# Streaming encoder step on one core: dense turns of one column group, additions to x and sums of squares on GpSimd, norms worked by group

## The reference

```python
def rmsnorm(x, gain):
    x32 = x.astype(F32)
    y = x32 * lax.rsqrt(jnp.mean(x32 * x32, axis=-1, keepdims=True) + EPS)
    return (y * gain.astype(F32)).astype(x.dtype)
...
    for l in range(DEPTH):
        ... mixer_inputs(rmsnorm(xp, norm1[l]), w_in[l], pos_p, lower[l])
        oa = diff_attn_prompt(aq, ak, av, lam)
        ob = dsa_prompt(bq, iq, iw, bk, bv, ik)          # top-256 keys of each query
        sc, oc = hgrn2_prompt(cq, ck, cg, cv)
        xp = xp + merge_heads(oa, ob, oc, cgate, lam_init, a_norm[l], c_norm[l], w_out[l])
        h, fc = conv_ffn(rmsnorm(xp, norm2[l]), hist0, ffn_up[l], ffn_conv_w[l], ffn_conv_b[l], ffn_down[l])
        xp = xp + h
    y_prompt = rmsnorm(xp, final_norm)
```

## Time and profile before

| | us |
|---|---|
| median of 3 runs | 4510.31 (4510.25 to 4512.2) |
| the profiled execution's own time | 4511.78 |
| its span | 4510.0 |
| PE busy / DVE busy / ACT busy / POOL busy | 4080.2 / 2281.9 / 996.6 / 224.3 |
| mean granted clock of TensorE | 0.919 |

### The profile page before, as it was taken

One profiled execution on the slowest core, in us unless ns is written; L12 is line 12 of the kernel. 1 busy time (PEld: TensorE's weight loads), 2 busy tenths in 40 slices (PEclk: granted clock), 3 DMA queues, 4 the chain that ended last, 5 costly groups with the idle time before them and its releaser, 6 DMA issues.

```text
span 4510.0 us, 47853 instructions
## 1 busy us (share of the span) xinstructions
PE 4080.2 (90%) x19244; PEld 2705.0 (60%) x19244; DVE 2281.9 (51%) x4647; ACT 996.6 (22%) x2287; POOL 224.3 (5%) x172
## 2 busy tenths in 40 slices
PE   7888788998889999998999998997899998899998
PEld 6665446776767767773444444486767776644443
DVE  1833454597942454439635555298924555522222
ACT  1113222110113333221223222011123332210001
POOL 2200220000000003100000000400000000000000
PEclk9995788999999999899998989998999998899999
DMA  3321122211120212221221211331121111122222
GB/s 127 109 91 31 53 64 90 77 66 47 52 84 18 69 61 73 87 84 70 70 74 49 73 56 55 108 110 56 45 79 54 47 55 56 37 85 65 77 75 73
DMA packets 142165, 310.33 MB, mean 69 GB/s; under 512 B 29160, under 2 KB 69608, under 8 KB 130680
## 3 DMA queue, kind: packets, MB, share of 16 engines
q1 hardware_dynamic: 81432, 262.25, 17.7%
q10 hardware_dynamic: 60512, 45.02, 3.5%
HBM read 271.08 MB, written 36.14 MB: 68 GB/s over the span
## 4 chain that ended last, share of the span: by engine, by line
PE 73%; DVE 19%; ACT 3%; issue 2%; DMA 1%; ACTq 1%; SPq 0%; DVEq 0%
PE PS L600 49%; PE PS L607 6%; DVE scr L1227 5%; DVE top L1226 5%; PE PS L698 4%; PE PS L687 3%; PE PS L671 3%; PE PS L657 2%; PE PS L576 2%; PE PS L794 1%; PE PS L725 1%; PE PS L793 1%; DVE inv L1164 1%; ACT scr L989 1%; DVE xn L1167 1%
## 5 line engine op out<-in xcount | busy, mean ns | idle before, releaser
L600 PE MATMUL PS<-xn,wring 128*128 128x272 f32 (+1 forms) x6048 | 1906.8, 477 | 74.1 <-DVE xn L1167 48.6
L600 PEld LDWEIGHTS PS<-xn,wring 128*128 128x128 f32 x6048 | 1188.2, 198 | 748.1 <-issue 552.6
L600 PE MATMUL PS<-dense,wring 128*128 128x272 f32 (+1 forms) x2112 | 681.3, 482 | 55.3 <-DVE xT L1173 45.9
L600 PEld LDWEIGHTS PS<-dense,wring 128*128 128x128 f32 x2112 | 417.2, 201 | 288.2 <-issue 217.2
L1173 DVE TENSOR_TENSOR xT<-PS,xT 128x272 f32<-128x272 f32 (+1 forms) x240 | 123.4, 523 | 499.0 <-PE PS L600 497.9
L1226 DVE MAX8 top<-scr 128x8 f32<-128x384 f32 (+6 forms) x418 | 367.5, 879 | 12.7
L1227 DVE MATCH_REPLACE8 scr<-top,scr 128x384 f32<-128x384 f32 (+6 forms) x418 | 359.9, 861 | 0.0
L607 PE MATMUL PS<-wring,xn 128*128 128x224 f32 (+1 forms) x1728 | 350.1, 364 | 10.5 <-ACT dense L865 10.5
L607 PEld LDWEIGHTS PS<-wring,xn 128*128 128x128 f32 (+1 forms) x1728 | 318.0, 187 | 35.5 <-ACT dense L865 11.2
L698 PE MATMUL PS<-kv,scr 128*128 128x64 f32 (+2 forms) x1804 | 249.5, 289 | 14.9 <-ACT scr L989 14.9
L698 PEld LDWEIGHTS PS<-kv,scr 128*128 128x128 f32 (+2 forms) x1804 | 237.6, 202 | 33.8 <-ACT scr L989 21.3
(11 more groups left out here) (160 smaller groups left out, 3090.8 us busy)
## 6 DMA issues: line engine op xcount, KB each, us to landing
wring<-in_wu SPq DMA_DIRECT2D x88, 1024.0 KB, 4.8
wring<-in_wf SPq DMA_DIRECT2D x76, 512.0 KB, 3.3
wring<-in_wd SPq DMA_DIRECT2D x64, 384.0 KB, 3.1
wring<-in_wn SPq DMA_DIRECT2D x24, 896.0 KB, 4.9
wring<-in_wd SPq DMA_DIRECT2D x64, 320.0 KB, 2.9
wring<-in_wo SPq DMA_DIRECT2D x32, 512.0 KB, 3.3
kv<-out_projT ACTq DMA_DIRECT2D x48, 256.0 KB, 4.3
out_projN<-dense SPq DMA_DIRECT2D x96, 112.0 KB, 1.7
```

The source lines that it names most:

```text
L600: mm = nc.tensor.matmul(PS[:, dbank(t.g0 + j), 0:cw], wtile(t.q, i), rhs, start=(kk == a), stop=(kk == b - 1))
```

## The change

- A turn works one column group (`j`), in both halves, and h = 1 is cut in two groups of 256.
- `f` begins with tiles 0, 1, 2 for group 0, then for group 1; later tiles take both groups in a row. `wo` and `dn` of pass 3 take all eight tiles for group 0 and then again for group 1, so that their weight tiles are loaded twice.
- ACT empties the banks of `wo` and `dn` as well, into two slots `res`; GpSimd adds them to x. In `wo` and in pass 3 of `dn`, GpSimd also squares the new x and adds the squares up over the eight tiles (in two tiles of `xn` that are free then). PE multiplies that one tile with a matrix of 1/1024. The norms at the start of P00 and P01 still square all eight tiles on ACT, now into `catT` (`direct`).
- The norm of group 0 stands before turn 3 of group 1 of the turns that add to x, and that of group 1 behind the first turn of the next stage that reads group 0.
- SP loads the 1/1024 matrix and the first half of x first, then three weight tiles, and then the constants and the other half.
- `LEAD` (dense turns ahead of the first mixer step) goes from 12 to 22, and a lag of 3 or 4 turns to 6, in a list of 974 turns where there were 542. `tout` has two slots where it had three.

```diff
-GRP = (((0, 272), (272, 272)), ((0, 512),))
+GRP = (((0, 272), (272, 272)), ((0, 256), (256, 256)))
+GMAX = 272
...
-NW, WSLOT = 3, 2048
+NW, WSLOT, NRES, NTO = 3, 2048, 2, 2
...
+def _norm(l, h, which, j, direct=0):
+    _turn("nsq", l, h, which, direct, j)
+    _turn("nsc", l, h, which, direct, j, ng=0)
...
 def _project(l, h):
-    _norm(l, h, 0)
-    for n in range(NPT):
-        _turn("f", l, h, n, load=("f", l, h, n, 0))
+
+    if l == 0:
+        _norm(l, h, 0, 0, 1)
+    for n, j in ((0, 0), (1, 0), (2, 0), (0, 1), (1, 1), (2, 1)) + tuple((n, j) for n in range(3, NPT) for j in range(2)):
+        _turn("f", l, h, n, 0, j, load=("f", l, h, n, 0))
+        if (n, j) == (0, 0):
+            _norm(l, h, 0, 1, 1 - l)
...
+def _added(kind, l, h, p, norm):
+
+    for j in range(2):
+        for n in range(KD):
+            _turn(kind, l, h, n, p, j, load=(kind, l, h, n, p))
+            if (n, j) == (2, 1):
+                _norm(*norm, 0)
 
 
 def _ffn(l, h):
-    for n in range(KD):
-        _turn("wo", l, h, n, load=("wo", l, h, n, 0))
-    _norm(l, h, 1)
-    ups = iter(range(NF))
+    _added("wo", l, h, 0, (l, h, 1))
     for p, upto in enumerate((8, 14, 19, 22)):
         for n in range(upto):
             if n >= (0, 8, 14, 19)[p]:
-                _turn("a", l, h, n, load=("u", l, h, n, 0))
-                _turn("g", l, h, n, load=("u", l, h, n, 0))
-        for n in range(KD):
-            _turn("dn", l, h, n, p, load=("dn", l, h, n, p))
+                order = ("a", 0), ("a", 1), ("g", 0), ("g", 1)
+                for kind, j in (("a", 0), ("g", 0), ("a", 1), ("g", 1)) if n == 0 else order:
+                    _turn(kind, l, h, n, 0, j, load=("u", l, h, n, 0))
+                    if (kind, n, j) == ("a", 0, 0):
+                        _norm(l, h, 1, 1)
+        if p < 3:
+            for n in range(KD):
+                for j in range(2):
+                    _turn("dn", l, h, n, p, j, load=("dn", l, h, n, p))
+    _added("dn", l, h, 3, (1, h, 0) if l == 0 else (L, h, 2))
...
 def _finish(h):
-    _norm(L, h, 2)
+    _norm(L, h, 2, 1)
     _turn("y", L, h, ng=0)
...
         def bank_free(pe, g):
-            if g >= 2:
-                by, n = EMPTIED[g - 2]
-                pe.wait_ge(s_ea if by == "act" else s_ed, n)
+            pe.wait_ge(s_ea, max(0, g - 1))
...
-            for t, name in ((ident, "ident"), (ones, "ones"), (lmask, "lmask"), (bmask, "bmask"), (fgain, "fgain"), (clow, "clow"),
-                            (par, "params")):
-                sp.eng.dma_start(t[:], io[name]).then_inc(s_const, 16)
-            sp.eng.dma_start(scr[:, 0:256].rearrange("p (l c) -> p l c", l=L), io["lam"]).then_inc(s_const, 16)
+            sp.eng.dma_start(mean[:], io["mean"]).then_inc(s_mean, 16)
             for k in range(KD):
-                sp.eng.dma_start(xT[:, k, :], io["xT"][k * P:(k + 1) * P, :]).then_inc(s_x, 16)
+                sp.eng.dma_start(xT[:, k, 0:W[0]], io["xT"][k * P:(k + 1) * P, 0:W[0]]).then_inc(s_x[0][k], 16)
+
+            def load_rest():
+                for t, name in ((par, "params"), (fgain, "fgain"), (clow, "clow"), (ident, "ident"), (lmask, "lmask"), (bmask, "bmask")):
+                    sp.eng.dma_start(t[:], io[name]).then_inc(s_const, 16)
+                sp.eng.dma_start(scr[:, 0:256].rearrange("p (l c) -> p l c", l=L), io["lam"]).then_inc(s_const, 16)
+                for k in range(KD):
+                    sp.eng.dma_start(xT[:, k, C0[1]:T], io["xT"][k * P:(k + 1) * P, C0[1]:T]).then_inc(s_x[1][k], 16)
...
-                    N = norm_index(k)
-                    for kk in range(KD):
-                        pe.wait_ge(s_sq, KD * N + kk + 1)
-                        for j, (c, cw) in enumerate(GRP[t.h]):
-                            if kk == 0:
-                                bank_free(pe, t.g0 + j)
-                            mm = nc.tensor.matmul(PS[:, dbank(t.g0 + j), 0:cw], ones[:], sq[:, kk % 2, c:c + cw],
-                                                  start=(kk == 0), stop=(kk == KD - 1))
-                            if kk == KD - 1:
-                                mm.then_inc(s_mm, 1)
-                        if kk < KD - 1:
-                            mm.then_inc(s_sqf, 1)
+                    c, cw = GRP[t.h][t.j]
+                    out = PS[:, dbank(t.g0), 0:cw]
+                    bank_free(pe, t.g0)
+                    if t.p:
+                        for kk in range(KD):
+                            pe.wait_ge(s_sq, KD * norms_before(k) + kk + 1)
+                            mm = nc.tensor.matmul(out, mean[:], catT[:, kk, c:c + cw], start=(kk == 0), stop=(kk == KD - 1))
+                    else:
+                        pe.wait_ge(s_acc, norms_before(k) - 4 + 1)
+                        mm = nc.tensor.matmul(out, mean[:], xn[:, SUM, c:c + cw], start=True, stop=True)
+                    mm.then_inc(s_mm, 1)
...
+                if t.kind == "nsq" and t.p:
                     for kk in range(KD):
...
+                        act.wait_ge(s_x[t.h][kk], 16)
+                        nc.scalar.activation(catT[:, kk, c:c + cw], xT[:, kk, xcols(t.h, c, cw)], ACT.Square).then_inc(s_sq, 1)
...
+                    act.wait_ge(s_xn, KD * (norms_before(k) - 1))
+                    act.wait_ge(s_mm, z.g0 + 1)
+                    nc.scalar.activation(inv[:, c:c + cw], PS[:, dbank(z.g0), 0:cw], ACT.Sqrt, bias=epst[:]).then_inc(s_ea, 1)
+                elif t.kind in ("wo", "dn"):
+                    i = ADDS[k]
+                    act.wait_ge(s_res, max(0, i - NRES + 1))
+                    act.wait_ge(s_mm, t.g0 + 1)
+                    nc.scalar.activation(res[:, i % NRES, 0:cw], PS[:, dbank(t.g0), 0:cw], ACT.Copy).then_inc(s_ea, 1)
...
+                    c, cw = GRP[t.h][t.j]
+                    dve.wait_ge(s_ea, TURNS[k - 1].g0 + 1)
+                    step(nc.vector.reciprocal(inv[:, c:c + cw], inv[:, c:c + cw]))
+                    dve.wait_ge(s_mm, last_user(k - 1))
                     dve.wait_ge(s_y, 16 * sum(1 for x in TURNS[:k] if x.kind == "y"))
                     gain = fgain[:] if t.n == 2 else par[:, t.l, (P_N1, P_N2)[t.n]:(P_N1, P_N2)[t.n] + KD]
                     for kk in range(KD):
+                        nc.vector.scalar_tensor_tensor(xn[:, kk, c:c + cw], xT[:, kk, xcols(t.h, c, cw)], gain[:, kk:kk + 1], inv[:, c:c + cw],
                                                        ALU.mult, ALU.mult).then_inc(s_xn, 1)
...
-                elif t.kind in BY_DVE:
-                    for j, (c, cw) in enumerate(GRP[t.h]):
-                        dve.wait_ge(s_mm, t.g0 + j + 1)
-                        x = xT[:, t.n, xcols(t.h, c, cw)]
-                        nc.vector.tensor_tensor(x, PS[:, dbank(t.g0 + j), 0:cw], x, ALU.add).then_inc(s_ed, 1)
...
+                if t.kind in ("wo", "dn"):
+                    c, cw = GRP[t.h][t.j]
+                    x, i = xT[:, t.n, xcols(t.h, c, cw)], ADDS[k]
+                    pool.wait_ge(s_ea, t.g0 + 1)
+                    pool.wait_ge(s_xn, KD * norms_before(k))
+                    nc.gpsimd.tensor_tensor(x, x, res[:, i % NRES, 0:cw], ALU.add).then_inc(s_res, 1)
+                    if t.kind == "wo" or t.p == 3:
+                        total, here = xn[:, SUM, c:c + cw], xn[:, SUM + 1, c:c + cw]
+                        pool.wait_ge(s_res, i + 1)
+                        if t.n == 0:
+                            pool.wait_ge(s_y, 16 * sum(1 for z in TURNS[:k] if z.kind == "y"))
+                            own(nc.gpsimd.tensor_tensor(total, x, x, ALU.mult))
+                        else:
+                            own(nc.gpsimd.tensor_tensor(here, x, x, ALU.mult))
+                            ins = nc.gpsimd.tensor_tensor(total, total, here, ALU.add)
+                            if t.n == KD - 1:
+                                ins.then_inc(s_acc, 1)
+                            else:
+                                own(ins)
+                if t.kind != "f" or FT[t.n][2] == 0 or t.j == 0:
```

239 lines of the change are left out of this document (100 added, 139 removed).

## The result

4249.18 us in the median of 4 runs (4246.33 to 4266.09) against 4511.26 of the kernel before in the same comparison: ratio 0.9426, 95% interval 0.9401 to 0.9451, 262 us faster. The forecast was 4350 (4265 to 4450): right in direction, too small by 100 us, outside its range. The profiled execution has a span of 4246.6 us at a mean granted clock of 0.941.

A forecast was written before the change was run, and what follows sets the result against it. It took TensorE, busy 4080 of 4510 us, to bound the kernel. Norms, start and end -105, additions -50, clock and finer weaving -35 and costs +30 made -160 us: 4350 us, range 4265 to 4450.

The forecast's parts named there:

- signs of being right: Listed observations: no addition waits, normed-tile waits under 25 us, GpSimd 0.74 us, 0.216 us at 256 columns, clock near 0.94.
- Clock and finer weaving: TensorE's clock over 400 us worth 16 us, as much again for other norms and alternating mixer steps: -35 us.
- -50 of the 66: Additions moved to GpSimd: of TensorE's 66.0 us of waits for them, 50 us gained, since late DVE still holds ACT.
- Sum -86 us: Norms covered by dense turns: gains of 7 to 14 us each, -86 us in all.
- start and end -105: Norms -86, start -11, P01's norm -3 and end -5 us together: -105 us.
- Net -11: Kernel start: first projection product at 23 us instead of 36.8, less 4.4 us for group 1's squares: -11 us.
- Groups of 256: Second half's 512 columns as two groups: 0.216 us an instruction, two making 0.432 against 0.429, so +7 us.
- GpSimd and the port, +5 and +8: GpSimd's chain showing in F01 and F11, +5 us; DVE waiting at the port for GpSimd's operations, +8 us.
- costs reckoned for dn's pass 3: GpSimd's 2.5 us chain against 2.3 us turns: 3 us, and 2 more waiting for group 0's norm.
- GpSimd as the bound: Slower rival: 272-column operations at 1.5 us outlast wo and dn's pass 3, +206 us, 4556 us; chance 0.07.
- Half eaten: Rival: DVE's lateness moves to the tanh and norms, so additions, norms and clock give less: about 4430 us; chance 0.20.
- More than the sum: Rival: the attention steps at 330 to 468 us keep 2.4 GHz: 4300 us, or 4285 with all additions; chance 0.15.

The follow-up runs named there:

- e15: Kernel before with only its group of 512 columns split into two of 256 in the same turn, order untouched: 4547.22 us, ratio 1.0087.
- e14: Kernel before with the 256-column split, turns of one group and the change's lag and lead; norms and additions as before: 4422.36 us, ratio 0.9814.
- e1: Changed kernel with mixer steps only behind every second dense turn (or any turn of rows), as coarse as before: 4374.09 us, ratio 0.9695.
- e3: Changed kernel with VectorE again adding the products of wo and down into x; squares and their sums stay on GpSimd: 4378.10 us, ratio 0.9699.
- e4: Changed kernel with three parts taken back: coarse order, no cover of norms, additions on VectorE: 4496.50 us, ratio 0.9969.
- e13: Changed kernel with coarse order and no cover of norms, but additions still on GpSimd: 4367.85 us, ratio 0.9686.
- e2: Changed kernel with both groups normed together behind the last turn of wo and of the last down-projection: 4255.03 us, ratio 0.9424.
- e7_double: Changed kernel with each GpSimd operation for additions, squares and sums done twice, the second into a spare buffer: 4364.96 us, ratio 0.9684.

## Why the forecast was too small, point by point

The runs price the change part by part: split +42 (e15), finer order -125 (e14 against e15, e1 against the changed kernel), additions -129 (e3, and e4 against e13), start and the norm's new chain 4496.5 - 4547.2 = -51 (e4 against e15), cover between +6 (e13 against e1) and -6 (e2). With +6 they sum to -257: that much is no test, since e15, e4, e13, e1 and the changed kernel are a chain of steps from one kernel to the other, each run's time taken from the next. The test is that order and additions cost the same at two places each, and the cover nearly so.

Most of what the forecast named as signs of being right came true: the waits for additions gone, those for normed tiles under 25 us (16.1), GpSimd's operations and busy time, 0.216 us for 256 columns, the clock at 0.94. The first product at 27.3 us did not, nor did the norms' products near 11 us in all (10.7 for the one-tile ones, 28.5 with those of P00 and P01). The range was missed all the same, because no sign bore on the finer order or on VectorE's side of the additions.

**"Clock and finer weaving. ... -35."** The step that failed most. I priced the finer order as "as much again for the other norms and for mixer steps that now alternate", some 17 us out of the air, from no row. It is 125. With this term right and the others as they were, 90 of the 101 us would have been found. The rows that could have warned me were in the trace, in the view of the earlier trace rows, where attention waits for its own steps:

```profile
PE PS L687 <- ACT scr L989: 38.9, 49, 3.9
PE PS L687 <- DVE scr L1271: 34.5, 19, 3.4
...
PE PS L671 <- ACT scr L977: 26.1, 10, 5.5
```

That is 99.5 us which a turn in between can cover. In the changed kernel the three are 30.4, 19.1 and, for VectorE, 10.9 us: 39 less. The clock that comes back with waits was taken for 400 us of span: the granted clock went to 0.941 over the whole span, 115 us by the estimate above. It is the 0.94 that I named among the signs, and it did not go into the sum.

**"I take -50 of the 66."** It was -129. I discounted TensorE's waits because VectorE is the floor in FFN(0, 0). The runs show the reverse: VectorE idled for a third of those stretches while it waited for TensorE's products, and reached its floor only after. The 66.0 us were also those of whole turns; split, they are 87 to 96, so that part of the 129 makes good what the split had cost.

**"Sum -86 us" for norms, with start and end -105.** The stretches came out at about this size, but not by the mechanism that I priced. From the start of each `wo` or last down pass to the first turn that reads the norm, the eight stretches (the last to TensorE's end) are 93 us shorter than before; I had 86 for seven of them and 5 for the last. But the cover brings 6 of it. The rest is the short chain (one product, squares summed on the way) and the additions gone from VectorE there: with additions put back, no cover and the coarse order (e4_all_back), 44 us remain. So in the sum of the runs norms, start and end are worth 45 to 57 us, about half of the 105: the term was too large by some 50 us, and by luck this made up for as much of what the other two lacked.

**"Net -11" for the start.** Its own figures (36.8 - 23 - 4.4) make 9, and the first product is at 27.3 us, not 23. I put the squares at 15 and had TensorE follow them at full speed, but

```profile
15.79 0.16 DVE L1535 TENSOR_TENSOR omlb<-clow 128x3 f32<-128x3 f32 x1 [14.92 <-DMA scr<-in_lam]
...
17.04 2.65 ACT L859 ACTIVATE catT<-xT 128x272 f32<-128x272 f32 x8
...
17.59 6.53 PE L605 MATMUL PS<-catT,mean 128*128 128x272 f32 x16 [17.59 <-ACT catT L859]
...
27.29 6.80 PE L628 MATMUL PS<-xn,wring 128*128 128x272 f32 x16 [3.16 <-DVE xn L1179]
```

the squares start at 17.04 us, and their products take 6.53 us for 16, where 0.230 each make 3.7. Most of them start 0.45 us apart, as do the projection's from 27.3 to 31.0 us, where the granted clock is 0.50; so I read them as run at 1.2 GHz, though the clock's own row still has 1.00 at 17.5 to 24.2 us. The 9.5 us gained are lost again by the end of the `f` turns, which take 171 us for 155. The Trainium skill (TensorE: Matmul & The Clock Gate, Part 1) puts the ramp at under 1% of a typical kernel span for modelling. For the ramp at the start the trace agrees: 3 us on these products and as much on the next 16 (6.80 us). What is not small is what the clock costs in the rest of this kernel: by the profile's mean clock (1 - 0.941) x 4246.6 = 250 us, 6%, are lost at 1.2 GHz even after the change.

**"Groups of 256. ... +7."** TensorE's part was right (58 instructions on 256 columns in 12.68 us, 0.216 each once the end's 0.16 is off), but it stood for the whole. In the old kernel the split costs 42 us, most of it in VectorE's doubled additions (21 of the 23 us between the profiled executions). I had looked for the price on one engine. In the changed kernel the waits for additions aren't paid, since the additions have gone.

**GpSimd and the port, +5 and +8.** The operation was sized well. In the changed kernel (lines by form; mean ns of one before the last bar):

```profile
L1458 POOL TENSOR_TENSOR xT<-xT,res 128x272 f32<-128x272 f32 x160 | 133.3, 834 | 1624.4 <-ACT res L869 1588.0 <-DVE xn L1179 34.9
L1458 POOL TENSOR_TENSOR xT<-xT,res 128x256 f32<-128x256 f32 x160 | 120.4, 753 | 1238.5 <-ACT res L869 1211.9 <-DVE xn L1179 24.7
...
L1466 POOL TENSOR_TENSOR xn<-xT 128x272 f32<-128x272 f32 x56 | 36.7, 655 | 4.4
```

0.66 to 0.83 us against 0.74, busy 645 us against 630. The costs reckoned for dn's pass 3 did not show where nothing runs beside it: the last down pass of FFN(1, 1) takes 36.5 us with the covered norm's product in it, and 35.7 without, both with GpSimd's additions (e2_no_cover) and with VectorE's in the split old kernel (e15_old_split); GpSimd's sum is then 7.4 us behind TensorE's last product, where some 5 were reckoned. The 0.59 us by the Trainium skill (GPSIMD Engine Reference, "Elementwise — side-by-side cycle accounting") is near the squares' 0.66 and 0.2 us under the additions'. The advice of the Trainium skill (same page, "When to use GPSIMD") to leave elementwise sums to VectorE would here have cost the 129 us: right for the operation, wrong for the queue it stands in. What the port took was not measured by itself.

**The rivals.** GpSimd as the bound: tested by e7_double, not met; its 206 us are also not what its figures give (76 against wo's 59 and dn's 35 and 60 us make 182). Half eaten: its time did not come. TensorE's waits for ScalarE's copies of `a`, which VectorE's product holds, did rise from 18.7 to 32.7 us, but they are 34.5 with the additions on VectorE (e3_dve_adds), so they did not come from moving these. More than the sum (0.15) holds the measured time in its band of 4230 to 4290 us, but by luck, for its mechanism did not happen: the stretch of attention steps still runs at a clock of 0.52, and dealing it out moved nothing. I had put the chance of a larger gain on one place that didn't move, and none on the two terms that did.
